# The first tile's prompt attention joined with the sample attention, and the setup in two halves of the feature groups

## What is computed

```
def _adaln(x, c, norm_g, w_mod, b_mod):
    mod = silu(c) @ w_mod + b_mod                      # 3 x 1024: shift, scale, gate
    shift, scale, gate = split(mod, 3)
    return _rms(x, norm_g) * (1 + scale) + shift, gate

def _layer(x, c, conv_prev, attend, ...):
    h, gate = _adaln(x, c, norm_g, w_mod, b_mod)
    (u_h, u_b, u_c, z_a, q, k, v, qi, ki, wi, z_b, g_a, g_b) = split(h @ w_in)
    q, k = _rms(q, q_norm), _rms(k, k_norm)            # 8 query heads, 2 key heads of 128
    branch_a = (u_b * short_conv(u_c * u_h)) * silu(z_a)
    branch_b = attend(q, qi, wi, k, v, ki) * silu(z_b)
    merged = sigmoid(g_a) * (branch_a @ w_pa) + sigmoid(g_b) * (branch_b @ w_pb)
    return x + gate * (merged @ w_out)

# attend: scores = sum_i wi * relu(qi . kidx); the 256 best visible keys are kept;
# softmax(q . k / sqrt(128)) @ v over them. Prompt: keys 0..t. Samples: the pages and the new tokens.
```

## Time and profile before

| | us |
|---|---|
| median of 3 runs | 3273.41 (3273.33 to 3274.37) |
| the profiled execution, its time | 3271.7 |
| its span (first to last instruction) | 3269.9 |
| PE busy in the span | 3167.0 (97%) |
| DVE busy | 1872.9 (57%) |
| ACT busy | 1105.6 (34%) |
| POOL busy | 842.7 (26%) |
| granted PE clock, mean | 0.993 of full |

### The profile page before, as it was taken

One profiled execution on the slowest core, in us unless ns is written; L12 is line 12 of the kernel. 1 busy time (PEld: TensorE's weight loads), 2 busy tenths in 40 slices (PEclk: granted clock), 3 DMA queues, 4 the chain that ended last, 5 costly groups with the idle time before them and its releaser, 6 DMA issues.

```text
span 3269.9 us, 48112 instructions
## 1 busy us (share of the span) xinstructions
PE 3167.0 (97%) x18999; PEld 2749.2 (84%) x18999; DVE 1872.9 (57%) x3608; ACT 1105.6 (34%) x1956; POOL 842.7 (26%) x769
## 2 busy tenths in 40 slices
PE   5999999988999999999999999999999999999999
PEld 5999999946998888889887888889888788889987
DVE  4343696034724995025346999146527899957652
ACT  2445332335424221145235221144326322125431
POOL 2345775343530232011200331010210133010011
PEclk9999999999999999999999999999999999999999
DMA  7765677674775555640754556610473455650017
GB/s 269 255 219 200 226 260 271 246 262 144 260 246 169 181 193 201 228 137 21 268 187 134 194 194 208 230 63 13 173 227 121 150 193 196 219 196 9 11 33 239
DMA packets 262304, 592.52 MB, mean 181 GB/s; under 512 B 17437, under 2 KB 174295, under 8 KB 212418
## 3 DMA queue, kind: packets, MB, share of 16 engines
q1 hardware_dynamic: 251714, 551.70, 49.4%
q0 software_dynamic: 10368, 37.75, 3.3%
HBM read 448.93 MB, written 140.47 MB: 180 GB/s over the span
## 4 chain that ended last, share of the span: by engine, by line
PE 91%; ACT 2%; DVE 2%; DMA 1%; POOL 1%; SPq 1%; issue 1%; another core or an unknown queue 1%; ACTq 0%; DVEq 0%; POOLq 0%
PE ps L1089 85%; PE ps L1094 7%; DVE RS L1699 1%; DMA MW<-in_w_mod 0%; POOL BBL L2255 0%; DMA WR<-in_w_in 0%; DMA QU<-q_scratch 0%; ACT SC L866 0%; SPq L484 0%; SPq L467 0%; DVE XN L1632 0%; DVE BB L2002 0%; POOL H L2154 0%; ACT sKPT L889 0%
## 5 line engine op out<-in xcount | busy, mean ns | idle before, releaser
L1089 PE MATMUL ps<-HTH,WLH 128*128 128x512 f32 x3504 | 1127.9, 390 | 0.0
L1089 PEld LDWEIGHTS ps<-HTH,WLH 128*128 128x128 f32 x3504 | 657.9, 188 | 139.1 <-issue 5.0
L1089 PE MATMUL ps<-HTL,WLH 128*128 128x512 f32 x1752 | 682.1, 389 | 0.0
L1832 DVE TENSOR_SCALAR_CACHE_REDUCE JUNK<-SC,SMALL 128x384 bf16<-128x384 f32 (+13 forms) x392 | 579.7, 1479 | 15.6 <-POOL sSC L2180 1.7
L1089 PE MATMUL ps<-H,WLH 128*128 128x288 f32 x3504 | 479.9, 297 | 6.3 <-POOL WLH L2113 4.3
L1089 PEld LDWEIGHTS ps<-H,WLH 128*128 128x128 f32 x3504 | 470.5, 189 | 8.6 <-POOL WLH L2113 4.8
L1089 PEld LDWEIGHTS ps<-HTL,WLH 128*128 128x128 f32 x1752 | 329.2, 188 | 65.3
L1949 DVE CUSTOM_DVE_ANT_0 LP<-ps,SC,RQ 128x512 f32<-128x512 f32 (+3 forms) x320 | 201.8, 667 | 297.3 <-PE ps L1089 175.9
L830 ACT ACTIVATE T<-ps 128x512 f32<-128x512 f32 x192 | 115.3, 600 | 708.1 <-PE ps L1089 702.9
L2113 POOL TENSOR_TENSOR WLH<-WR,WLH 128x1024 fp32r<-128x1024 f32 x97 | 235.5, 2428 | 316.5 <-ACT WLH L671 316.5
L1089 PE MATMUL ps<-V,T 128*128 128x128 f32 x2176 | 286.8, 278 | 10.7 <-ACT T L966 10.7
(11 more groups left out here) (330 smaller groups left out, 4494.0 us busy)
## 6 DMA issues: line engine op xcount, KB each, us to landing
WLH<-w_scratch SPq DMA_DIRECT2D x291, 1024.0 KB, 4.8
w_scratch<-WLH SPq DMA_DIRECT2D x97, 1024.0 KB, 6.0
WR<-in_w_in SPq DMA_DIRECT2D x73, 512.0 KB, 4.4
MW<-in_w_mod SPq DMA_DIRECT2D x6, 2048.0 KB, 15.6
XN<-in_x_prompt SPq DMA_DIRECT2D x4, 2048.0 KB, 7.9
q_scratch<-QO SPq DMA_DIRECT2D x32, 256.0 KB, 5.6
ma_scratch<-T SPq DMA_DIRECT2D x32, 256.0 KB, 5.7
gb_scratch<-GB SPq DMA_DIRECT2D x32, 256.0 KB, 6.6
```

What stands on the lines that cost most here:

```text
L1089: return pe.matmul(out, lhsT, rhs, start=start, stop=stop, **more)
L1832: ins_ = dve.tensor_scalar(JUNK[0:n, 0:row.shape[1]], row, MID[0:n, c:c + 1], 0.0, ALU.is_ge, ALU.add, accum_out=CNT[0:n, c:c + 1])
```

## The change

It has three parts.

1. **Setup in halves.** The small loads go to ACT's queue. XN comes in four blocks with a semaphore each. The w_mod chunks are taken in the order 0, 2, 1, 3, 4, 5, so that shift and scale of the groups 0 to 3 are there first; half a product of weight tiles 0 and 1 is computed with them before chunks 1 and 3 are used, the other half after. Four buffers (HIN) take the place of two between `modulate` and the splits, and DVE makes the low parts of the odd groups. MW no longer overlaps H. `page_rows` (DVE) moves into PROJ_A.
2. **Early gathers.** The first seven page gathers are issued one every fourth item of PROJ_B instead of all at item 20.
3. **One attention loop** (`both_attentions`) on PE, ACT, DVE and POOL, with steps s = 0 to 22. Step s works on sample chunk (s / 4, s % 4) and on prompt unit k = s - LEAD = s - 5. Sample logits have one bank (0), from which DVE copies them to sL while it takes the maximum; sL is double, and exp works on it in place. Prompt units use banks 1 and 2 for logits, 3 for P, 4 as the one accumulator. LP0, the copies of P and BB get other places in SBUF, partly those of page buffers; 12 buffers remain in the rotation. Two of the w_proj_b weights are loaded and split near the end of the loop. The load of the next XN waits also for the last low parts of BB.

The diff, cut to its core:

```diff
-    use_slot = lambda n: n if n < 4 else n + 12 if n < 7 else (n - 3) % 16
-    use_ahead = lambda n: None if n < 19 else n - 16 if n - 16 >= 7 else n - 19
+    LEAD = 5
+    use_step = lambda what, u, c, e: 4 * u + c - 1 if what == "k" else 4 * u + c + 5
+    PAGE_SLOT, PAGE_AHEAD, PAGE_STEP = [0, 1, 2, 3, 16, 17, 18], [None] * 7, [None] * 7
+    turns_end = {x: (-1, None) for x in (*range(6, 12), *range(12, 16))}
+    turns_end[0], turns_end[16] = (use_step(*PAGE_USES[0]), 0), (use_step(*PAGE_USES[4]), 4)
+    for n in range(7, len(PAGE_USES)):
+        step = use_step(*PAGE_USES[n])
+        x = min((x for x in turns_end if step < 16 or x not in range(12, 16)), key=lambda x: turns_end[x][0])
+        PAGE_SLOT.append(x)
+        PAGE_STEP.append(max(turns_end[x][0], PAGE_STEP[-1] or -1))
+        PAGE_AHEAD.append(turns_end[x][1])
+        turns_end[x] = (step, n)
...
         load_x(0)
-        load_mw(0)
+        for q in (0, 2):
+            load_mw(q)
+        load_w(0)
         load_mw(1)
-        load_w(0)
-        load_mw(2)
         load_w(1)
         load_mw(3)
         load_w(2)
+        store_w(0)
+        load_mw(4)
+        store_w(1)
+        load_mw(5)
...
@@ PE: setup @@
+        modulation(0, 0)
+        modulation(2, 1)
+        turn_modulation(0, ps[7][:, 0:P])
+        turn_modulation(2, ps[7][:, 2 * P:3 * P])
+        turn_x(0, 0, 5)
+        turn_x(0, 1, 6)
+        turn_sample()
+        turn_x(0, 2, 5)
+        turn_x(0, 3, 6)
+        products(0, steps=FIRST_HALF)
+        modulation(1, 2)
+        pe.wait_ge(*mod_ready.at("AM", 0))
+        turn_modulation(1, ps[7][:, P:2 * P])
+        products(1, steps=FIRST_HALF)
+        turn_x(0, 4, 6)
+        claim(5)
+        modulation(3, 5)
+        turn_modulation(3, ps[7][:, 3 * P:4 * P])
+        freed[7] = mod_ready.at("AM", 1)
+        for k in (5, 6, 7):
+            turn_x(0, k, 6 - k % 2)
...
@@ PE: both_attentions @@
+            for s in range(len(UNITS) + LEAD + 2):
+                (u, c), after, k = divmod(s, 4), divmod(s + 1, 4), s - LEAD
+                late = (u - 1, c - 1) if c else (u - 2, 3)
+                if in_units(k):
+                    unit_logits(0, k)
+                if in_units(k - 2):
+                    turn_out(0, k - 2)
+                if u in PAIRS:
+                    logits(u, c)
+                if in_units(k - 1):
+                    for hh in range(2):
+                        pe.wait_ge(*expd.at(0, k - 1, hh))
+                    turn_p(0, k - 1, 0, 3)
+                if c == 1 and u - 2 in PAIRS:
+                    turn_back(u - 2)
+                if u - 1 in PAIRS:
+                    if c == 0:
+                        turn_probabilities(u - 1, 4)
+                    turn_probabilities(u - 1, c)
                 for x in range(4):
+                    if x == 2 and in_units(k - 1) and unit_groups(0, k - 1) > 1:
+                        turn_p(0, k - 1, 1, 3)
+                    if after[0] in PAIRS:
+                        keys(*after, x)
+                    if late[0] in PAIRS:
+                        values(*late, x)
+                    if x in (0, 3) and in_units(k - 1) and x // 3 < unit_groups(0, k - 1):
+                        group_values(0, k - 1, x // 3)
+                if c == 1 and u in PAIRS:
+                    logits(u, 4)
...
@@ POOL @@
+        def both_attentions():
+            for s in range(-1, len(UNITS) + LEAD + 2):
+                for n in range(7, len(PAGE_USES)):
+                    if PAGE_STEP[n] == s:
+                        gather_pages(n)
+                k = s - LEAD
+                if k >= 0 and in_units(k + 2):
+                    query_low(0, k + 2)
+                if s in (len(UNITS) + LEAD - 1, len(UNITS) + LEAD):
+                    split_low(AFTER_PAGES[s - len(UNITS) - LEAD + 1])
+                if s == len(UNITS) + LEAD:
+                    sample_low(0)
+            whole_keys(0)
...
@@ ACT: both_attentions, step s @@
+                if c == 0 and u - 1 in PAIRS:
+                    sample_turned(u - 1, 4)
+                if in_units(k - 1):
+                    copy_p(0, k - 1, 0)
+                if u - 1 in PAIRS:
+                    sample_turned(u - 1, c)
+                if after[0] in PAIRS:
+                    sample_keys_copy(*after, 0)
+                if in_units(k):
+                    exponentials(0, k)
+                if in_units(k - 1) and unit_groups(0, k - 1) > 1:
+                    copy_p(0, k - 1, 1)
+                if after[0] in PAIRS:
+                    sample_keys_copy(*after, 2)
+                if k >= 0 and in_units(k + 2):
+                    query_high(0, k + 2)
+                if c == 3 and u in PAIRS:
+                    sample_probabilities(u, 4)
+                    sample_probabilities(u, 0)
+                elif c < 3 and u - 1 in PAIRS:
+                    sample_probabilities(u - 1, c + 1)
...
@@ SP: load_x @@
             if t:
                 sp.wait_ge(*attn_z.at(t - 1, UNITS[-1]))
+                if t == 1:
+                    for k in (KC - 2, KC - 1):
+                        sp.wait_ge(*bb_ready_at(0, k, "P"))
...
@@ POOL: PROJ_B, item i @@
-                if t == 0 and i == SAMPLE_ITEMS + 4:
-                    for n in range(7):
-                        gather_pages(n)
+                if t == 0 and i >= SAMPLE_ITEMS + 4 and i % 4 == 0 and (i - SAMPLE_ITEMS - 4) // 4 < 7:
+                    gather_pages((i - SAMPLE_ITEMS - 4) // 4)
```

More of the change, by code:

```diff
@@ L1562, in _ @@
                 if t + 1 < TILES:
[L1563 removed]
+                    b = 4 + count[0] % around[0]
+                    count[0] += 1
+                    turn_x(t + 1, f, b)
                 j += 1
```

734 lines of the change are left out of this document (375 added, 359 removed).

## The result

Five runs each on one chip: before 3273.33 us (median; 3270.76 to 3274.37), after 3255.98 (3252.24 to 3258.73). The ratio is 0.9946 with a 95% interval of 0.9935 to 0.9958: 17.4 us off by the medians. The forecast was 3245 (3226 to 3263): inside the range, 11 us too low. The profiled execution of after took 3252.24 us, the shortest of the five (span 3250.4), so the two traces differ by 19.5 us where the medians differ by 17.4. Full clock is 2.4 GHz of TensorE's granted clock, half clock 1.2 GHz.

What follows compares the result with a forecast made beforehand. TensorE, busy 97% of 3269.9 us, was taken as the bound, with gains only where it idles or runs at half clock. 9 + 5 + 14.4 = 28.4 off 3271.7 gave 3243.3; the median stands 1.7 above: 3245 us, range 3226 to 3263.

Steps and rivals of the forecast that it cites:

- What bounds the kernel: TensorE busy 97%; gains only where it idles or runs at half clock: tile 0's setup, near 385 us, and attention.
- Setup, 9 us: Start of tile 0: second product ends near 59 us instead of 68.5; 9 us off, bounds 3 and 13.
- Early gathers, 5 us: Near 385 us: no weight split waits behind seven gathers on POOL; 5 us off, bounds 0 and 6.0.
- Attention, 14.4 us: Joined attention loop of tile 0, PE work unchanged: 180.3 us against 194.7, 14.4 off, bounds 0 and 25.
- Steps 0 to 4 and 5 to 15: Joined loop: first five steps without prompt work 41.4 us (47.9 before, bounds 36 and 48), the next eleven 88.5.
- Steps 16 to 20: Joined loop after the last sample logits: 10.2 + 20.9, plus 1.6 for a P copy, less 2.3: 30.4 us.
- Tail: Attention's end, from step 21: gets worse, 20 us against 13.7, PE idle some 8 and perhaps at half clock.
- XN's load at no cost: Next tile's XN load, later behind the last low parts: barely covered, costed at nothing, 0 to 3 us in range.
- Joined steps that bind each other (1): Attention: in-order queues and shared banks cost another 1.3 us in each of 11 steps; 3259 us, chance 0.15.
- Setup gives nothing (2): Setup: the last 2 MB come no earlier and DVE's low parts take 1.98 us; 3254 us, chance 0.10.
- a stall with each batch of four gathers (4): Steps 5 to 15: the unexplained stall comes with each batch, 11 x 5 = 55 us; 3300 us, chance 0.06.
- Signs named: Profile after: second product near 59 us, no wait near 375, attention 180 us, BB's low parts last, PE idle 6 to 10.

Runs made afterwards that it cites:

- after_small_first: The changed kernel with its eight small loads back on SP ahead of XN, as before the change; median 3256.48 us, ratio to before 0.9943.
- before_spread: The kernel before with only the seven early gathers issued one every fourth item; median 3267.81 us, ratio to before 0.9986.
- after_tail_fill: The changed kernel with 56 identity transposes on PE between the attention's last turn and the first w_proj_b product; median 3256.22 us, ratio to before 0.9948.

## Why the prediction was right, and by how much it was off

- **What bounds the kernel**, right: everything came from the three places named, and tiles 1 to 3 didn't change (m4 to the end +1.5 us, within the scatter of 2377.9 to 2384.6).
- **Setup, 9 us.** At the second product's end it is 68.5 - 59.6 = 8.9. The 2.8 us for the small loads hold (after_small_first). The low parts on DVE took 1.64 and 1.67 us, not 1.5, its casts 0.41 to 0.59, not 0.96, so a half's chain took 5.3 us and not 6.8; the half clock over the last 48 matmuls, which I had not priced, took 2.6 back. That the end agrees to 0.6 us is in part luck. The Trainium skill, SBUF — State Buffer, Who interferes with whom, holds that DVE and GpSimd lock each other out, DVE with two SBUF inputs and also with a cast in its two-port mode. The trace agrees in both: in after a difference of two SBUF tiles with 512 columns takes DVE 0.68 us at 58.02 us, with POOL idle (64 partitions), and 1.64 beside POOL's low parts; a cast takes 412 to 594 ns with four low parts on POOL and 935 to 1508 with eight. I had weighed only the first half of the rule. Missed: behind the second product TensorE ran 3.4 us at half clock (63.1 to 66.5 us), and a wait of 0.81 us near 179 us. Left at m1: 6.6 by the two traces, 5.4 to 8.4 over all profiles of after's setup against before and before_spread.
- **Early gathers, 5 us** (0 to 6): 6.1, 5.7 alone, 3.4 to 5.8 when undone. Right.
- **Attention, 14.4 us.** This is the term that was mis-sized: 8.0 to m3, 8.3 to m4, and 7.2 to the end of the first product, where its sum ends (187.5 us against 180.3). By sort of time, against before: idle time and half clock fell by as much as the whole term, and PE's own work grew by 6.4 us at full clock, where the prediction has "PE work is unchanged" (and 2.5 for hand-offs and 1.6 for a copy). By its own steps, another account of the same miss:
  - Steps 0 to 4 and 5 to 15: 33.6 and 94.0 us, forecast 41.4 and 88.5. The sum, 127.6 against 129.9, came out right, in part by luck; the border wasn't right, since the window of before up to 700.6 held six sample steps, not five, and the next one ten, not eleven. From that next window I took 6.0 us of waits where PE had 3.4 idle and 3.4 at half clock (1.7 lost), 5.1 at most: at the 5.02 us of 706.2 TensorE itself stood still for 1.53. Like for like, from m2 to the logits of step 5, it went from 41.9 to 34.4 us; the stall and the half clock behind it are most of that.
  - Steps 16 to 20: 34.9 against 30.4. TensorE is busy 31.9 us, where I had 31.1; but I took off 2.3 for work that falls into the tail and had no idle time but 1.6. There are 3.0 us of it, 1.8 of them (0.3 to 0.9 us a step) at the values, which wait for the one accumulator bank, which `finish` frees behind both `mask_logits` on DVE.
  - Tail: 25.0 against 20, from 802.5 to the end of the first product at 827.5. whole_keys took 4.67 us instead of 3.4, and I said that PE may drop to half clock but gave it no price: the first product took 9.1 us instead of after_tail_fill's 6.5.
- **XN's load at no cost**, right in the changed kernel, where TensorE ran through the next stage (48.5 of 48.5 us), and right that it is barely covered: with the tail mended the fourth or the fifth weight tile is late by 4.8 or 3.0 us behind it.
- **Rivals.** Joined steps that bind each other (1): TensorE is busy 91.5 of 93.9 us in them, so no. Setup gives nothing (2) and a stall with each batch of four gathers (4): not seen; in the joined steps no gap exceeds 0.7 us. But a step that costs a busy PE more work, as the 6.4 us above show, wouldn't be seen as idle time.
- **Signs named**: second product 59.6 (59 named), no wait near 375, PE idle 8.8 us in the tail (6 to 10), low parts last on the chain: as named. From its start the stage took 178.2 us to the first product's start and 187.5 to its end, where 180 was named.

What the forecast lacked beside that is the look one stage further. As the loads stand, a shorter attention shows little at m4: the stage behind it has its DMA engines busy 0.97 of the time, and 4.7 us taken out of the tail came back there to within 0.1. With XN's load dealt out, m2 to m4 is 14.3 us shorter than before (225.0 against 239.3), so it was the order of the loads and not their volume that stood in the way up to there.

## What to carry to other kernels

Before pricing a gain, read the DMA share of the stage behind it: where it is near 1, a stage that starts sooner can wait longer for its weights, until a large load is dealt out between the small ones that somebody waits for (6 us at m4 here, none in the medians). Interleaving two streams of matmuls isn't free for the engine that runs them: compare its busy time at full clock, not its idle time alone (6.4 us here). Take step borders from the instructions, not from a window that looks right, and price the half clock behind every idle stretch that you forecast. A work split between DVE and GpSimd moved the end of the chain by 1.0 us here, and nothing behind it. And take more than one profile of each kernel before a stage's few us are believed.

## What the runs showed of the hardware that I had not expected

- While software-issued gathers go out back to back (1.24 us each), TensorE stalls near the end of the row: 6.39 us with 16 (in both profiles), 0.5 to 2.3 us with 11, 3.6 us over a row of eight that came soon after another. The stall moved with the row.
- DVE's 128x512 cast took 412 to 594 ns on average with four of POOL's subtractions in the setup and 935 to 1508 ns with eight; the subtraction itself took POOL 1.28 to 1.46 us either way. I had expected the cast's time to be its own.
- 14 to 56 identity transposes in a wait kept TensorE's granted clock at 1.0 (half clock gone at 32.4, 49.5 and 810.6 us, though 6.8 us of it came at 59.4). It bought 2.8 us at the end of the second product, and nothing in the medians.
- Waits of 1.8 to 2.5 us on TensorE are followed by 3.4 us at half clock in some profiles and by none in others of the same code (near 351, and some 550 and 1666 us behind m4). Such a stretch costs 1.7 us, and the three are much of the scatter between profiles.
- The same 1420 matmuls cost TensorE some 144.7 us at full clock in two stages of their own and 151.1 joined step by step (estimates, from busy time and the time at half clock). The cause isn't shown.
